# Turned tokens, tables and bias laid out by the host, and a new order of the first loads and splits

## The chip, the cores and the metric

The kernel runs on one core of one Trainium2 chip. The metric is the device time of one execution in microseconds (us), the median of several runs. Engines are named as the profile names them: PE is TensorE (its weight loads are PEld), DVE is VectorE, ACT is ScalarE, POOL is GpSimd, SP is SyncE, which here only issues DMAs.

## The reference

One sequence of 256 tokens, width 1024, fp32 throughout. Two blocks follow each other.

The first block: RMS norm, one projection of 3088 columns, gated linear attention with 4 heads and a block attention with 8 heads, an output projection, RMS norm, and a retrieval layer: 8 heads each take the top 16 of 128 x 128 product keys, gather the 16 rows of `peer_u` and `peer_v` for each token (4 KB a row), and add `gate * gelu(u.x) * v`.

```
x = first_block(x, ...)
  xn = rmsnorm(x, norm1_w); proj = xn @ w_in
  o_gla, o_moba from proj;  x += concat(o_gla, o_moba) * mix_scale @ w_out
  q = rmsnorm(x, norm2_w) @ w_query; s = q . subkeys; top-16 of 128, twice; top-16 of 256
  x += sum_k gate_k * gelu(u_k . xn) * v_k
x = second_block(x, ...)
  twice: mixer, then conv-GLU feed-forward (1024 -> 2 x 2816 -> 1024), then
         x += sigmoid(rmsnorm(x) @ ple_gate) * (p @ ple_proj)
```

The mixer of the second block's first layer is stick-breaking attention beside HGRN2; that of its second layer is a sliding-window attention whose logits get a bias from a table of 32 distance buckets for each of 16 heads. The feed-forward's convolution has three taps and a bias for each column.

## The kernel before, in words

All matrix products are done in two halves of a number: an operand is split into `hi` (rounded, type fp32r) and `lo = x - hi`, and `product` sums three matmuls, hi*hi, hi*lo and lo*hi (lines L2093 to L2095). Weights arrive as pieces of 1 MB (128 partitions x 2048 numbers) in four slots. A piece goes through a fixed chain: SP loads it (`load`, L468), ACT rounds it to `hi` (`split`, L436), DVE (`split_lo`, L443) or POOL (`split`, L591) makes `lo`, PE uses it. A slot is loaded again when the old piece's `hi` and `lo` are made, and rounded again when PE has used the old piece. Each engine works through one list written out by hand, in order; `PLAN` gives each PE job a number, its PSUM bank is that number modulo 8, and `pe_done` and `evac_done` count the jobs.

The tokens' root of the mean square is not needed before the products: it is multiplied in when a product is taken from PSUM (`root_col`, L1338).

The start, in the order of PE's list: the norm weights, loaded as 72 rows by six DMAs of ACT's queue, are turned (L2157); the 256 x 1024 tokens are turned by 16 transposes (`norm_T`, L2058); eight spins (L2052, matmuls with no use but to keep PE at work); the first projection tile of both halves of the tokens (`dense_tile("win", 0, t)`), the 16-column gate projection ("gr"), the turning of the convolution's taps (L2171), the one-hot product that spreads the bias table (L2174), then win tile 1 of the first tokens, alpha (L2179), win tile 1 of the second tokens, and so on. ACT meanwhile takes the squares and roots of the tokens (`norm_root`, L801 to L811), rounds the turned tokens (L832), and the pieces.

Six projection chunks of two pieces each are made: pieces 0 and 1 are split by DVE, 2 and 3 by POOL, 4 and 5 by DVE, 6 and 7 by POOL, 8 to 11 by DVE. DVE's list: `early_tables` (takes gr, taps and bias row, and waits for the constants and for eight small tables that SP broadcasts to all partitions, `gain_loaded`), the splits of 4 and 5, `gla_gate`, `gla_log_gate` and the query norms and rotation `moba_qk` (L1395 to L1418), the splits of 8 and 9, the same for the keys, the splits of 10 and 11.

The bias row of 16 heads is written out 128 times to a scratch tensor in device memory (L499) and read back skewed at the second layer (L570). The sub-keys are loaded in their own layout and turned by PE in four jobs ("subk", "subk_rest"), copied by DVE (L1574) and ACT (L946). The side input `p` is turned by PE at the end of each feed-forward (job "pT", `ple`), copied from PSUM to `PHI` and subtracted into `PLO` by DVE (L1940, L1941). There POOL makes `lo` of the side projection's weights (`ple_proj_lo`, L591).

## Time and profile before

| | |
|---|---|
| median of 3 runs | 1551.3 us (1549.95 to 1555.15) |
| the profiled execution | 1546.3 us |
| its span, first to last instruction | 1544.5 us |
| PE, DVE, ACT, POOL busy | 90, 67, 46, 40% of the span |
| DMA moved | 415 MB, 269 GB/s on average |

The profile is of one execution. A row of the timeline gives the start, the length and the instruction with how often it follows itself; a row of the chain of waits gives one step of the work that ended last.

### The profile page before, as it was taken

The numbers are of one execution on the slowest core, as the hardware profiler recorded it, in microseconds if no ns is written. First come the engines' busy times: TensorE is split into PE (matmuls) and PEld (weight loads), VectorE is DVE, ScalarE is ACT, GpSimd is POOL, SyncE is SP. The second block draws the span as 40 slices with busy tenths as digits, with TensorE's granted clock in tenths as the row PEclk, the third lists the DMA queues.
The fourth block names the chain that finished last, engine by engine and source line by source line (L and its number), as shares of the span: only waits on it lengthen the run. The fifth ranks groups of instructions, "written<-read, shape, count | busy, mean of one in ns | idle before, by whom it ended". The sixth has DMA issues, their size and how long they took to land.

```text
span 1544.5 us, 18260 instructions
## 1 busy us (share of the span) xinstructions
PE 1388.1 (90%) x5985; PEld 969.8 (63%) x5985; DVE 1028.5 (67%) x1916; ACT 711.6 (46%) x1381; POOL 620.2 (40%) x581
## 2 busy tenths in 40 slices
PE   7989998787788867778789999999999999999998
PEld 6877973333333323333335879788888778888887
DVE  4895786666666766666664547669863586498733
ACT  5534643233322333333334372477645755776534
POOL 2330777433433333333362521045443512364414
PEclk9999999889999999998899999999999999999999
DMA  9287599999999999999999601557665443476650
GB/s 312 89 138 231 211 339 411 421 422 421 422 422 422 421 422 422 422 421 422 421 413 348 198 32 50 164 165 217 190 218 175 162 139 104 125 207 195 215 192 28
DMA packets 187076, 415.00 MB, mean 269 GB/s; under 512 B 9882, under 2 KB 113922, under 8 KB 160386
## 3 DMA queue, kind: packets, MB, share of 16 engines
q0 software_dynamic: 43776, 268.45, 42.4%
q1 hardware_dynamic: 143090, 145.66, 30.8%
q8 instruction: 38, 0.62, 0.2%
q14 instruction: 28, 0.23, 0.0%
q10 hardware_dynamic: 144, 0.04, 0.0%
HBM read 409.93 MB, written 4.19 MB: 268 GB/s over the span
## 4 chain that ended last, share of the span: by engine, by line
PE 51%; DMA 21%; DVE 10%; ACT 6%; POOL 6%; issue 5%; ACTq 0%; POOLq 0%; DVEq 0%; SPq 0%
DMA expert_rows<-in_peer_uv,route_idx 20%; PE ps L2380 10%; PE ps L2549 10%; PE ps L2093 7%; PE ps L2095 7%; PE ps L2094 7%; PE ps L2550 5%; DVE weights_lo L443 2%; POOL expert_rows L674 2%; POOL weights_lo L591 2%; ACT weights_hi L436 2%; PE ps L2058 1%; DMA weights_raw<-in_ab_w_in 1%; POOL ple_proj_lo L591 1%; ACT scratch L981 1%
## 5 line engine op out<-in xcount | busy, mean ns | idle before, releaser
L1677 DVE CUSTOM_DVE_ANT_0 expert_rows<-expert_rows,ps 128x1024 f32<-128x1024 f32 x184 | 224.1, 1220 | 147.0 <-DMA expert_rows<-in_peer_uv,route_idx 131.7
L591 POOL TENSOR_TENSOR weights_lo<-weights_raw,weights_hi 128x512 fp32r<-128x512 f32 x120 | 160.0, 1366 | 370.2 <-ACT weights_hi L436 328.1
L2380 PE MATMUL ps<-expert_rows,scratch 128*128 128x512 f32 x512 | 246.2, 639 | 58.4 <-ACT scratch L981 55.0
L674 POOL DMA_INDIRECT expert_rows<-in_peer_uv,route_idx x156 | 147.3, 944 | 225.9 <-PE ps L2380 189.6
L436 ACT CAST weights_hi<-weights_raw 128x2048 fp32r<-128x2048 f32 x98 | 185.5, 1917 | 106.4 <-PE ps L2095 79.8
L2380 PEld LDWEIGHTS ps<-expert_rows,scratch 128*128 128x128 f32 x512 | 102.1, 204 | 201.6 <-issue 124.6
L2549 PE MATMUL ps<-x_normT,weights_hi 128*128 128x512 f32 x640 | 222.5, 393 | 0.0
L443 DVE TENSOR_TENSOR weights_lo<-weights_raw,weights_hi 128x2048 fp32r<-128x2048 f32 x68 | 160.9, 2373 | 74.2 <-ACT weights_hi L436 73.8
L2093 PE MATMUL ps<-weights_hi,x_normT 128*128 128x512 f32 (+1 forms) x496 | 188.3, 380 | 9.3 <-DVE weights_lo L443 3.7
L967 ACT ACTIVATE proj<-proj 128x4 f32<-128x4 f32 x64 | 13.2, 205 | 397.8 <-DVE proj L1677 397.8
L2095 PE MATMUL ps<-weights_hi,x_normT 128*128 128x512 f32 (+1 forms) x496 | 184.7, 372 | 0.0
L2094 PE MATMUL ps<-weights_lo,x_normT 128*128 128x512 f32 (+1 forms) x496 | 184.6, 372 | 0.0
L2550 PE MATMUL ps<-x_normT,weights_lo 128*128 128x256 f32 x640 | 178.3, 279 | 0.0
L2380 PE MATMUL ps<-expert_rows,proj 128*128 128x512 f32 x288 | 135.7, 627 | 25.7 <-ACT proj L981 25.1
L2549 PEld LDWEIGHTS ps<-x_normT,weights_hi 128*128 128x128 f32 x640 | 119.9, 187 | 27.1
L2380 PEld LDWEIGHTS ps<-expert_rows,proj 128*128 128x128 f32 x288 | 56.6, 200 | 104.1 <-issue 68.8
L2550 PEld LDWEIGHTS ps<-x_normT,weights_lo 128*128 128x128 f32 x640 | 120.6, 188 | 0.0
L2093 PEld LDWEIGHTS ps<-weights_hi,x_normT 128*128 128x128 f32 x496 | 93.4, 188 | 31.0 <-issue 4.2
L2095 PEld LDWEIGHTS ps<-weights_hi,x_normT 128*128 128x128 f32 x496 | 93.4, 188 | 16.6
L2094 PEld LDWEIGHTS ps<-weights_lo,x_normT 128*128 128x128 f32 x496 | 93.5, 189 | 15.5 <-issue 0.2
L2380 PE MATMUL ps<-work_a,proj 128*128 128x512 f32 x112 | 65.5, 739 | 36.3 <-ACT proj L981 36.3
L1905 DVE SCALAR_TENSOR_TENSOR work_a<-ps,conv_cols,work_a 128x254 f32<-128x254 f32 (+1 forms) x176 | 76.4, 475 | 29.3 <-ACT work_a L1120 25.1
(365 smaller groups left out, 2452.5 us busy)
## 6 DMA issues: line engine op xcount, KB each, us to landing
weights_raw<-in_ffn_up SPq DMA_DIRECT2D x88, 512.0 KB, 5.0
weights_raw<-in_ffn_down SPq DMA_DIRECT2D x22, 1024.0 KB, 4.9
weights_raw<-in_ab_w_in SPq DMA_DIRECT2D x14, 1024.0 KB, 6.0
weights_raw<-in_w_in SPq DMA_DIRECT2D x12, 1024.0 KB, 8.0
weights_raw<-in_ple_gate SPq DMA_DIRECT2D x8, 1024.0 KB, 6.2
weights_raw<-in_c_w_in SPq DMA_DIRECT2D x6, 1024.0 KB, 5.9
weights_raw<-in_w_out SPq DMA_DIRECT2D x4, 1024.0 KB, 12.8
weights_raw<-in_peer_w_query SPq DMA_DIRECT2D x4, 1024.0 KB, 12.5
```

The costliest lines, as they stand in the source:

```text
L436: copy(w.hi[:, :], w.raw[:, :]).then_inc(hi_ready[w.h], 1)
L443: eng.tensor_tensor(w.lo[:, :], w.raw[:, :], w.hi[:, :].bitcast(F32), ALU.subtract).then_inc(lo_ready[w.h], 1)
L591: ins = pool.tensor_tensor(w.lo[:, c], w.raw[:, c], w.hi[:, c].bitcast(F32), ALU.subtract)
L674: nc.gpsimd.indirect_dma_start(out=dst, out_offset=None, in_=table, in_offset=bass.IndirectOffsetOnAxis(ap=r_idx[:, q, n:n + 1], axis=0)). ...
L1677: ins = nc.vector.tensor_tensor_reduce(out=rows, in0=rows, in1=tokens, scale=1.0, scalar=0.0, op0=ALU.mult, op1=ALU.add, accum_out=r_dot[: ...
L1905: ins = nc.vector.scalar_tensor_tensor(out=d, in0=PS[:, (j0 + 2 * q + g) % 8, 0:S - n], scalar=CONV[:, l, bass.ds(i * RING + (tap * 2 * FT ...
L2093: pe.matmul(o, x[0], w[0], start=first, stop=False)
L2094: pe.matmul(o, x[0], w[1], start=False, stop=False)
L2095: return pe.matmul(o, x[1], w[0], start=False, stop=last)
L2380: ins = pe.matmul(PS[:, (J[f"peer_{t}"] + m) % 8, :], DIAG[b][:, k, :], rows[:, m * BANK:(m + 1) * BANK], start=False, stop=False, skip_gr ...
L2549: pe.matmul(b.rearrange("p (a t) -> p a t", a=2), hi[:, c, g, :], x_both(c), start=c == 0, stop=False)
L2550: ins = pe.matmul(b[:, 0:S], lo[:, c, g, :], XHI[:, c, :], start=False, stop=c == KC - 1)
```

## The change

The host prepares seven arrays (`laid_out`): the tokens turned (1024 rows of features), the norm weights as 72 columns, the taps and their bias as columns, the sub-keys turned, `p` turned, the whole banded window bias (128 x 16 x 256), and the table of `u` and `v` rows side by side, which was there before. On the chip the turnings by PE, their copies out of PSUM, the scratch tensor and its write are gone.

- Start: SP loads turned tokens in two halves, then win pieces 0 to 3, then the tokens in rows, then gr, alpha and all constants, then pieces 4 and 5, then the taps, the eight broadcast tables, the levels and pieces 6 to 11. ACT's queue has one DMA in place of six.
- ACT rounds the turned tokens (8 instructions of 128 x 256), then pieces 0 and 1 in quarters of 512 columns, then pieces 2 and 3 whole, then squares and roots, then the 16-column weights, then 4 and 5. DVE follows with the quarters of `lo`.
- PE: six matmuls on the turned tokens whose result is overwritten, then the first tile, each step as its quarter becomes ready.
- POOL splits pieces 2, 3 and 7; DVE splits 6, ahead of `gla_log_gate`.
- alpha goes to two banks, one for each half of the tokens.
- `PHI` and `PLO` are made from the loaded `p` in SBUF.
- The sub-keys' load goes ahead of the wait for `mb_O1`, and query piece 5 no longer waits for PE's turning of the sub-keys. The second layer's bias is one plain load.

```diff
-            sp.dma_start(C[:, 0:P], a["c_small"][:, 0:P]).then_inc(sem("ident_loaded"), 16)
-            for t in range(TT):
-                sp.dma_start(X[:, t, :], a["x"][0, t * P:(t + 1) * P, :]).then_inc(sem(f"x_loaded{t}"), 16)
+            for half in range(2):
+                cols = slice(4 * half, 4 * half + 4)
+                sp.dma_start(XCOLS[:, cols, :], a["x_cols"][:, cols, :]).then_inc(sem(f"x_cols_loaded{half}"), 16)
             for p in halves(0):
                 load("win", p)
+            for p in halves(1):
+                load("win", p)
+            for t in range(TT):
+                sp.dma_start(X[:, t, :], a["x"][0, t * P:(t + 1) * P, :]).then_inc(sem("x_loaded"), 16)
             sp.dma_start(W_GR, cols512(w_in, 1536, GRANK)).then_inc(sem("gr_loaded"), 16)
             sp.dma_start(W_ALPHA, a["gla_w_alpha"][0]).then_inc(sem("gr_loaded"), 16)
-            for p in halves(1):
+            sp.dma_start(C[:, :], a["c_small"]).then_inc(sem("const_loaded"), 16)
+            for p in halves(2):
                 load("win", p)
...
-            for p in (*halves(1), *halves(3)):
+            for p in (2, 3, 7):
                 split("win", p)
...
+            act.wait_ge(sem("vec_loaded"), 16)
+            for f in range(KC):
+                if f % 4 == 0:
+                    act.wait_ge(sem(f"x_cols_loaded{f // 4}"), 16)
+                nc.scalar.activation(XHI[:, f, :], XCOLS[:, f, :], ACT.Copy,
+                                     scale=VEC[:, NORM_COL[0] + f:NORM_COL[0] + f + 1]).then_inc(sem("first_hi"), 1)
+            for half in halves(0):
+                w = pieces["win", half]
+                act.wait_ge(raw_loaded[w.r], w.landed)
+                for c in range(4):
+                    cols = slice(c * BANK, (c + 1) * BANK)
+                    act.copy(w.hi[:, cols], w.raw[:, cols]).then_inc(hi_ready[w.h] if c == 3 else sem("first_hi"), 1)
+            for p in halves(1):
+                split("win", p)
             for t in range(TT):
-                norm_root(0, t, (sem(f"x_loaded{t}"), 16), (sem(f"x_loaded{t}"), 16))
...
+                norm_root(0, t, (sem("x_loaded"), 32), (sem("x_loaded"), 32))
...
             def moba_queries():
+                split_lo(v, "win", 6)
                 gla_log_gate()
                 moba_qk(0)
...
-                j = J[f"pT{l}"]
-                src = bank(j).rearrange("p (c t) -> p c t", c=2)
-                step(nc.vector.tensor_copy(PHI[:, :, :], src))
-                freed(nc.vector.tensor_tensor(PLO[:, :, :], src, PHI[:, :, :].bitcast(F32), ALU.subtract), j)
+                v.wait_ge(sem("p_loaded"), 16 + 16 * l)
+                step(nc.vector.tensor_copy(PHI[:, :, :], PIN[:, l]))
+                nc.vector.tensor_tensor(PLO[:, :, :], PIN[:, l], PHI[:, :, :].bitcast(F32), ALU.subtract).then_inc(sem("p_split"), 1)
...
+            b = bank(tile_job("win", 0, 0))
+            pe.wait_ge(sem("x_cols_loaded0"), 16)
+            for _ in range(6):
+                pe.matmul(b[:, 0:S], XCOLS[:, 0, 0:P], XCOLS[:, 0, :], start=True, stop=True)
+            for f in range(KC):
+                w, c = pieces["win", f // 4], f % 4
+                pe.wait_ge(*((lo_ready[w.h], w.count) if c == 3 else (sem("first_lo"), KC + 3 * (f // 4) + c + 1)))
+                hi, lo = part(w.hi, 4), part(w.lo, 4)
+                ins = product(b, xs(f, slice(0, P)), (hi[:, c, :], lo[:, c, :]), f == 0, f == KC - 1)
+            ins.then_inc(pe_done, 1)
+            dense_tile("win", 0, 1)
```

## Rows read from the trace of the kernel before

**Rows 1.** The page: shares of the span in the chain of waits, by engine.
```profile
PE 51%; DMA 21%; DVE 10%; ACT 6%; POOL 6%; issue 5%; ACTq 0%; POOLq 0%; DVEq 0%; SPq 0%
```

**Rows 2.** Stage table: stretch, length, busy us of each engine, PEclk, DMA share, GB/s.
```profile
4.00:11.00 7.00, 2.59 (x13) 2.62 (x14) 0.53 (x3) 5.75 (x19) 0.00 (x0) 1.00 1.05 392
...
20.00:24.00 4.00, 4.00 (x20) 3.30 (x19) 1.89 (x4) 1.35 (x1) 4.00 (x4) 1.00 0.35 72
...
300.00:800.00 500.00, 394.02 (x818) 163.02 (x817) 335.64 (x842) 155.08 (x501) 193.53 (x206) 0.92 1.01 421
```

**Rows 3.** Timeline, the first tokens' work and gr: start us, length us, engine, line.
```profile
5.54 0.63 ACT L801 ACTIVATE x_norm<-x_res 128x512 f32<-128x512 f32 x1 [0.58 <-DMA x_res<-in_x]
...
8.55 3.62 PE L2058 MATMUL ps<-consts,x_res 128*128 128x128 f32 x16
...
8.95 0.29 ACT L811 ACTIVATE stats<-stats 128x1 f32<-128x1 f32 x1
...
17.34 0.41 ACT L855 CAST w_gr_hi<-scratch 128x128 fp32r<-128x128 f32 x1
...
19.18 0.43 SPq L492 DMA_DIRECT2D sink_rows<-in_sinks  x1
...
20.26 0.88 DVE L1378 TENSOR_TENSOR w_gr_lo<-scratch,w_gr_hi 128x128 fp32r<-128x128 f32 x1
```

**Rows 4.** Chain of waits, 0 to 60 us: start us, length us, what.
```profile
26.82 0.12 PE ps L2093
...
29.63 0.30 PE ps L2171 x4
...
30.68 0.43 PE ps L2093
```

**Rows 5.** DMA issues, 0 to 215 us: KB each, us from issue to landing.
```profile
sink_rows<-in_sinks SPq DMA_DIRECT2D x1, 8.0 KB, 6.3
```

**Rows 6.** Timeline of DVE and ACT, 28 to 90 us.
```profile
43.19 0.75 DVE L1338 TENSOR_SCALAR proj<-ps,stats 128x512 f32<-128x512 f32 x1 [3.69 <-PE ps L2095]
...
48.91 1.70 DVE L1404 TENSOR_TENSOR proj<-proj,stats 128x512 f32<-128x512 f32 x1
...
58.84 0.69 DVE L1404 TENSOR_TENSOR proj<-proj,stats 128x512 f32<-128x512 f32 x1
...
62.55 1.41 DVE L1338 TENSOR_SCALAR proj<-ps,stats 128x512 f32<-128x512 f32 x2
63.88 4.48 DVE L443 TENSOR_TENSOR weights_lo<-weights_raw,weights_hi 128x2048 fp32r<-128x2048 f32 x2
...
43.17 3.72 ACT L436 CAST weights_hi<-weights_raw 128x2048 fp32r<-128x2048 f32 x2 [1.07 <-PE ps L2095]
```

**Rows 7.** Timeline of POOL, 18 to 90 us: the splits of pieces 2, 3 and 6, 7.
```profile
19.69 10.08 POOL L591 TENSOR_TENSOR weights_lo<-weights_raw,weights_hi 128x512 fp32r<-128x512 f32 x8 [19.23 <-ACT weights_hi L436]
45.23 12.50 POOL L591 TENSOR_TENSOR weights_lo<-weights_raw,weights_hi 128x512 fp32r<-128x512 f32 x8 [15.46 <-ACT weights_hi L436]
```

**Rows 8.** Timeline of the first side input, DVE and (last row) one POOL instruction.
```profile
1198.24 0.67 DVE L1940 CAST ple_hi<-ps 128x512 fp32r<-128x512 f32 x1
1198.95 0.69 DVE L1941 TENSOR_TENSOR ple_lo<-ps,ple_hi 128x512 fp32r<-128x512 f32 x1
1200.04 3.08 DVE L443 TENSOR_TENSOR weights_lo<-weights_raw,weights_hi 128x2048 fp32r<-128x2048 f32 x1 [0.40 <-ACT weights_hi L436]
...
1200.93 3.34 POOL L591 TENSOR_TENSOR ple_proj_lo<-ple_proj_raw,ple_proj_hi 128x512 fp32r<-128x512 f32 x1
```

**Rows 9.** Chain of waits at the first side input.
```profile
1199.73 7.05 POOL ple_proj_lo L591 x4
```

**Rows 10.** Timeline: PE behind the sub-keys and behind the side input, first gather.
```profile
163.36 0.36 PE L2093 MATMUL ps<-weights_hi,x_normT 128*128 128x256 f32 x1 [0.29 <-DVE x_normT L1325]
...
173.51 1.11 POOL L661 DMA_INDIRECT expert_rows<-in_peer_u,route_idx  x1 [4.38 <-DVE route_idx L1639]
...
1194.65 0.47 PE L2093 MATMUL ps<-weights_hi,x_normT 128*128 128x512 f32 x1 [0.34 <-DVE x_normT L1325]
```

More of the change, by code:

```diff
@@ L1368, in _ @@
             step(nc.vector.memset(SS[:, 95:96], EPS), "eps_ready")
-            freed(nc.vector.tensor_copy(VEC[:, :], bank(J["vecs"])[:, 0:72]), J["vecs"], wait=True)
+            for f in range(KC):
+                v.wait_ge(sem("first_hi"), f + 1)
+                nc.vector.scalar_tensor_tensor(out=XLO[:, f, :], in0=XCOLS[:, f, :],
+                                               scalar=VEC[:, NORM_COL[0] + f:NORM_COL[0] + f + 1],
+                                               in1=XHI[:, f, :].bitcast(F32), op0=ALU.mult,
+                                               op1=ALU.subtract).then_inc(sem("first_lo"), 1)
+            for half in halves(0):
+                w = pieces["win", half]
+                for c in range(4):
+                    cols = slice(c * BANK, (c + 1) * BANK)
+                    v.wait_ge(*((hi_ready[w.h], w.count) if c == 3 else (sem("first_hi"), KC + 3 * half + c + 1)))
+                    nc.vector.tensor_tensor(w.lo[:, cols], w.raw[:, cols], w.hi[:, cols].bitcast(F32),
+                                            ALU.subtract).then_inc(lo_ready[w.h] if c == 3 else sem("first_lo"), 1)
             for t in range(TT):
@@ L1372, in _ @@
             v.wait_ge(sem("norm_rstd"), rstd_no[0])
-            for half in range(2):
-                norm_lo(0, 0, (half,))
-                split_lo(v, "win", half)
-            norm_lo(0, 1)
             v.wait_ge(sem("gr_hi_ready"), 1)
@@ L1878, in vec_ffn @@
                 norm_lo(k, 1)
+                v.wait_ge(sem("conv_loaded"), 16)
                 j0 = J[f"up{l}"]
@@ L2297, in _ @@
             spin(J["wout"], 3)
-            def subkeys(j, m):
-                pe.wait_ge(sem("subkeys_loaded"), 16)
-                transposes(j, [SKN[:, 4 * m + n, :] for n in range(4)])
             def head_tokens(t, j):
@@ L2594, in ple @@
             def ple(l, k):
-                pe.wait_ge(sem("p_loaded"), 16 + 16 * l)
-                transposes(J[f"pT{l}"], [PIN[:, l, t, c * P:(c + 1) * P] for c in range(2) for t in range(TT)])
                 dense_tile(f"gate{l}", 0, 0, normed(k, 0))
```

148 lines of the change are left out of this document (49 added, 99 removed), and 4 rows, old and new, of the table PLAN.

## The prediction

> **What bounds the kernel now.** I read the shares of the chain of waits first. PE carries half of it and DMA a fifth [rows 1], so the span is made of stages with different owners. The table by stage shows that from 300 to 800 us the DMA engines are full, share 1.01 at 421 GB/s [rows 2]: this is the gather of expert rows, which the change does not touch. Its first gather is issued at 173.5 us, when the first indices are there [rows 10]. Whatever the change gains or loses ahead of that point moves the gather as a block, and the rest with it; behind it only the edits at the side inputs count. So there are two questions: how much sooner the indices come, and what happens at 1200 and 1516 us.
>
> Ahead of the gather the chain is PE from 26.8 us on without a pause [rows 4], then from about 62 us DVE: it takes the product of win chunk 2 only at 62.55 us, though PE had it earlier, because it was in the query norms from 43.19 us on [rows 6]. The end of win tile 1 at E = 42.9 us (just ahead of the 43.19 row) is the hinge: I work out how E moves, then how long DVE needs from E to its 62.55.
>
> **The start, to win tile 1.** Before, gr starts at 26.82, ends at 29.63, taps and bias row take to 30.68, and then win tile 1 starts [rows 4]. In the changed kernel the first tiles come sooner, but I find that they don't set the time. gr needs the 16-column weights in two halves, and on ACT these now stand behind the roots of the tokens, and the tokens' rows load behind four pieces. Bytes up to the last token row: 1 MiB turned tokens + 4 MiB pieces + 1 MiB rows = 6.29 MB. At the 392 GB/s of 4 to 11 us [rows 2], with 2.0 us until the first byte, the last arrives at 2.0 + 16.1 = 18.1. Before, 64 KB of constants and half a MiB had to arrive for the first root at 5.54 [rows 3]: 2.0 + 0.59 MB / 392 = 3.5, so up to 2 us between byte and use; I take 1.5: 19.6. The two roots took 5.54 to 9.24, 3.7 us; the hi 0.41, the lo 0.88 [rows 3]: 24.6, PE at 24.7. gr is 2.8 long: 27.5, and nothing is left between it and win tile 1. So tile 1 starts at 27.5 in place of 30.68: **-3.1 us** (bounds -4 and -1.5, from a lag of 0.6 to 3.1 us).
>
> Do the two first tiles end ahead of 24.7? The turned tokens land near 5 us; the norm columns, one DMA, by about 6. Eight roundings of about 0.4, then quarters of half a us as piece 0 and 1 land (2.1 and 3.1 MB: near 9 and 12 us), lo behind them: PE begins near 12, is fed the last quarter near 16, and is through both tiles (48 matmuls of 0.227, the spacing in the chain) near 23. Two us of slack. POOL has piece 2 from about 16.5 on; at 10.08 for two pieces [rows 7] both are ready at 27, in time for the first and second half of tile 1. So all of the chunked start, its early norm table and the six extra matmuls cost and bring nothing here: the roots hide them.
>
> **The small tables, later now.** The eight broadcasts stood ahead of pieces 4 and 5 and now stand behind them. Before, the last was issued at 19.18 and took 6.3 us [rows 3, 5]: 25.5, at a time when DMA was nearly empty, share 0.35 over 20 to 24 [rows 2]; so they are slow by themselves. DVE waits for all eight ahead of its splits of 4 and 5. After: gr, alpha, constants, pieces 4 and 5 are 2.9 MB behind the rows, with taps end of bytes near 26, then 4 to 5 us for the eight. I take G = 30.6. Behind G on DVE: two splits 4.6, one evacuation 0.75, gate 0.87, absolute value 0.69; on ACT two functions and a table load 2.6: G + 9.5. ACT can only round piece 6 behind it, and PE frees its slot at E = 39.8. So G matters from 30.3 on, one for one; **+0.5 us** (bounds 0 and +2).
>
> **Piece 6 from POOL to DVE.** Before, from 43.19 to 62.55, DVE is 19.4 us, of which one and the same instruction of the query norms takes 1.70 us beside POOL's splits and 0.69 when POOL is done [rows 6, 7]. Reading it as waiting for the POOL instruction under way fits: each of the six instructions beside POOL is about one us longer. With 6 on DVE, POOL has 4 instructions in place of 8. But DVE must wait for ACT's hi (1.9 behind the hinge) and work 2.29 (half of the 4.48 row) ahead of everything, until E + 4.4; POOL's four for piece 7 (ready at E + 3.8) then alternate with DVE's next ones (log gate, scaling, square), each of which waits 1.25 until POOL's is through. From E: 4.4, then 6.2, 7.9, 10.3, sums to 11.8, root and reciprocal 12.3, two halves of norm and rotation 3.7 each: 19.7. Before it was 19.6. **0 us**: split and saved waits cancel. Bounds: +0.3, and -2.8 if nothing waits for POOL any more (6.2 us of waits gone, 3.4 us of split and its wait added). I stay at the upper end, since the alternation is what the 1.70 row shows. PE's list behind it (chunks 2 to 4, until about E + 36) stays ahead of DVE, as before.
>
> The Trainium skill (SBUF — State Buffer, "Who interferes with whom") says that DVE and GpSimd take a shared pair of ports as an exclusive lock: an instruction of DVE with two SBUF inputs, or a plain copy in a two-port mode, waits for a GpSimd one that reads SBUF, or the other way round, for its whole length. The rows agree: 1.70 is 0.69 plus most of a POOL instruction. By that rule the term is 0; by a view in which the engines share bandwidth it would be negative.
>
> **The side inputs.** POOL's four instructions on the side projection are on the chain, 7.05 us [rows 9], and again at the second side input, where the row is alike. Without a wait they would take 5.04, as half the 10.08 of rows 7; the rest is one of 3.34 us that sat behind DVE's split of 3.08 [rows 8]. Before, DVE's two instructions ahead of it (0.67 and 0.69) read PSUM, and POOL passed beside them. After, both read SBUF alone. The copy waits for POOL's instruction, 0.2, runs about 0.35; POOL's last on the gate piece starts that much late, ends near 1200.0; the subtraction waits for it, runs to 1200.7; POOL's first of four starts there in place of 1199.7; DVE's split waits for that, runs to 1204.2; POOL's other three end at 1208.0, where they ended at 1206.8. **+1.2 at each, +2.4 in all**; bounds 0 (no wait at all) and +1.3 each. As DVE and POOL may fall into a better order, I take 1.0 each: **+2.0 us**. PE had 0.3 us or less to spare there. By the skill's rule the copy from SBUF takes the pair as well; if it did not, the subtraction alone would cost 0.7 to 0.9 each.
>
> **Edits at nothing.** The sub-keys' turning: PE waited 0.29 us for DVE's norm behind it, ahead of the query products [rows 10], so that wait hides it; 0. The turning of `p`: PE waited 0.34 for DVE behind it [rows 10]; 0. The scratch write and the bias load have no waiter in the chain; the plain load is of the same size, 2 MB. DVE's and ACT's copies of the sub-keys stood ahead of waits for PE. Query piece 5's earlier load: its hi waits for PE, not for the load. alpha in two banks: 0. The sub-keys' load stands ahead of query piece 4 on SP, 1 MB or 2.6 us of DMA, in a stretch with no wait for pieces.
>
> **Sum.** -3.1 + 0.5 + 0 + 2.0 = -0.6 us on the execution of 1546.3; on the median of 1551.3, which is 5.0 above it and has the same stages, that is 1550.7. Extremes: -4.0 - 2.8 = -6.8, and -1.5 + 2.0 + 0.3 + 2.6 = +3.4. A measurement of this kernel tells about 0.3%, 4.7 us, from no change.
>
> **Rivals.**
> - **POOL and DVE do not get in each other's way as I say.** Then piece 6 brings -2.8 and the side inputs cost 0: -3.1 + 0.5 - 2.8 = -5.4, 1545.9. For it: POOL's instructions halve beside the norms, and 1.0 us each was paid there six times. Against it: the 3.34 row, and that the split has to be worked off somewhere. If the lag of the rows is short too, 1545.0.
> - **The tables come late and DVE becomes the bound from there (slower).** Place: DVE's wait for the eight tables ahead of the splits of 4 and 5. From G = 30.3 each us counts; break-even with the start's gain, side inputs included, is at G = 31.4 (-3.1 + 2.0 = -1.1 to be eaten), and at G = 36 the sum is -1.1 + 5.7 = +4.6, 1555.9. For it: they needed 6.3 us with an empty DMA, and are now queued behind 2 MB of pieces. Against it: SP issues them well ahead of their bytes, so that most of this runs beside the pieces' bytes.
> - **PE's clock stays low.** Before, the 16 transposes take 3.62 us, 0.226 each [rows 3], the spacing of the lower level (1.2 GHz), before the products run at the upper one; the granted clock column shows 1.00 all the same. After, PE has a pause ahead of the products, waits between quarters, and waits 2 us ahead of gr. If the two tiles and gr all ran at the lower level, 48 matmuls of 0.454 and 24 of 0.234 from 12 us on, win tile 1 would start at 39.4, +8.7, in all +10.7 with the side inputs: 1562. It decides once the level rises later than about 2 us, the slack, behind the first product. The skill (TensorE: Matmul & The Clock Gate, "HAM oscillation — how this bites in real kernels") says that pauses of PE bring back the half rate; here the pauses are short, so I give it little.
> - **The start gains more:** the roots of the tokens don't hold gr. Then tile 1 starts near 26 and the sum is -2.
>
> **Chances.** My forecast and the small variants around it (1547 to 1553, its own range) 0.60; the first rival 0.22; late tables 0.12; low clock 0.04; something not listed 0.02. Faster by over 0.3%: most of the first rival and a tail of the forecast, 0.27. Slower by over 0.3%: half of the late tables' cases, the clock, a tail of the forecast: 0.13. Within 0.3%: 0.60. The range takes in the first rival's time and the upper sum: 1544.5 to 1555.0.
>
> **What would show it.** Win tile 1 starting near 27.5 us, with PE waiting some 2 us ahead of gr for DVE's lo of the 16-column weights; if PE doesn't wait there, the first step is wrong. DVE's wait for the tables ending between 29 and 32. DVE taking chunk 2 about 19.7 us behind the end of win tile 1: 2 or 3 us sooner speaks for the first rival. The first gather at about 171 in place of 173.5. POOL's four side-projection instructions ending 1 us later than their place in the stage before, twice. If the first gather comes at 168 or sooner, the prediction is wrong in the start; if the stretch from first gather to end is shorter than before, it is wrong in the side inputs or in an edit that I priced at nothing.

## The result: slower by some 5 us, and the profile after

The kernel after takes 1555.8 us (median of 10 runs) against 1551.4 us: ratio 1.0033 with a 95% interval of 1.0022 to 1.0044. A second comparison gave 1.0039 [1.0026, 1.0053]. That is 3.4 to 8.2 us slower; the forecast was 1550.7 us, no change, with a range of 1544.5 to 1555.0. Two executions far outside the rest, 3216 us (x_first, below) and 1739 us (before), were marked slow and are in no ratio.

The two profiled executions are further apart than the medians, 1556.7 us with a span of 1554.9 against 1546.3 and 1544.5. Before reading anything from that, it has to be known what one kernel does from one execution to the next; the first two experiments are on that.

The page of after, shares of the chain of waits [rows 1]:

```profile
PE 47%; DMA 21%; DVE 10%; POOL 7%; ACT 7%; issue 6%; SPq 1%; another core or an unknown queue 0%; POOLq 0%; DVEq 0%; ACTq 0%
```

PE has lost 4 points, and SP's issuing, at 0 before, has 1. Part of that is the start, where the chain no longer runs over PE. The chain of waits of after from 0 to 70 us, at the places where [rows 4] had PE alone (start, length, what):

```profile
8.87 7.25 SPq L490
...
23.23 13.00 DMA sink_rows<-in_sinks
...
38.52 2.28 DVE weights_lo L453
...
42.27 0.70 DVE work_a L1442
...
45.58 1.81 ACT weights_hi L446
47.51 2.29 DVE weights_lo L453
...
61.75 0.70 DVE proj L1410
```

Up to 23 us the chain is SP's own issues, one of which (the alpha weights, behind the 1024 short rows of the 16-column weights) held it for 7.25 us; then it is the last of the eight small tables, 13.0 us from issue to landing where [rows 5] had 6.3; then it is DVE's list, with ACT's two functions and one split between. PE, which was the chain here before, is not in it at all.

The timeline of after: ScalarE, PE and then DVE, which answer to [rows 3, 4, 6] (start, length, instruction, idle time before it and what ended that):

```profile
19.76 0.63 ACT L801 ACTIVATE x_norm<-x_res 128x512 f32<-128x512 f32 x1 [1.00 <-DMA x_res<-in_x]
...
25.14 0.29 PE L2093 MATMUL ps<-x_normT,w_gr_hi 128*16 128x256 f32 x1 [3.79 <-DVE w_gr_lo L1387]
29.50 0.40 PE L2093 MATMUL ps<-weights_hi,x_normT 128*128 128x512 f32 x1
...
23.76 1.32 DVE L1387 TENSOR_TENSOR w_gr_lo<-scratch,w_gr_hi 128x128 fp32r<-128x128 f32 x1
...
36.30 4.49 DVE L453 TENSOR_TENSOR weights_lo<-weights_raw,weights_hi 128x2048 fp32r<-128x2048 f32 x2 [6.19 <-DMA sink_rows<-in_sinks]
...
47.51 2.29 DVE L453 TENSOR_TENSOR weights_lo<-weights_raw,weights_hi 128x2048 fp32r<-128x2048 f32 x1 [3.75 <-ACT weights_hi L446]
49.72 1.78 DVE L1446 SCALAR_TENSOR_TENSOR work_a<-work_a 128x512 f32<-128x512 f32 x1
...
57.31 0.69 DVE L1409 TENSOR_TENSOR proj<-proj,stats 128x512 f32<-128x512 f32 x1
...
64.73 1.41 DVE L1339 TENSOR_SCALAR proj<-ps,stats 128x512 f32<-128x512 f32 x2
```

Win tile 1 starts at 29.50 instead of 30.68, so the start without the turnings did bring PE 1.2 us. But DVE stands idle until 36.30 for the tables, and takes chunk 2 at 64.73 us instead of 62.55 [rows 6]. The first gather follows at 175.53 instead of 173.51 [rows 10].

The stage table of after, to set beside [rows 2] (stretch, length, busy us of each engine, PEclk, DMA share, GB/s):

```profile
24.00:28.00 4.00, 2.86 (x15) 2.01 (x16) 2.40 (x3) 2.81 (x2) 2.23 (x2) 0.68 0.90 311
28.00:32.00 4.00, 4.00 (x22) 3.14 (x21) 0.41 (x1) 2.27 (x2) 0.00 (x0) 0.89 0.16 45
32.00:36.00 4.00, 4.00 (x18) 2.91 (x16) 0.00 (x0) 0.00 (x0) 0.00 (x0) 1.00 0.47 166
...
300.00:800.00 500.00, 389.28 (x813) 160.90 (x812) 336.74 (x849) 153.00 (x493) 192.88 (x204) 0.93 1.01 421
```

While DVE waits for the tables, the DMA engines are busy for 16 and then 47% of the time and move 45 and then 166 GB/s: the stream stands, though the engines are mostly idle. The first and the last of the eight, in the list of DMA issues of after (KB, us from issue to landing):

```profile
gain_rows<-in_gla_out_norm_w SPq DMA_DIRECT2D x1, 64.0 KB, 8.3
...
sink_rows<-in_sinks SPq DMA_DIRECT2D x1, 8.0 KB, 13.0
```

They were issued at 19.30 and 23.23 us, so they landed at 27.6 and 36.2: the eight took 8.6 us. The gather from 300 to 800 us is the same as before.

At the first side input, DVE of after and then its chain of waits, beside [rows 8, 9]:

```profile
1207.11 0.52 DVE L1942 CAST ple_hi<-work_b 128x512 fp32r<-128x512 f32 x1
1207.66 1.67 DVE L1943 TENSOR_TENSOR ple_lo<-work_b,ple_hi 128x512 fp32r<-128x512 f32 x1
...
1208.79 7.48 POOL ple_proj_lo L591 x4
```

The subtraction takes 1.67 us beside POOL instead of 0.69. From SP's load of the side input to its first load of `c_w_out` is 66.87 us (1174.10 to 1240.97) instead of 66.30 (1165.22 to 1231.52); from the second such load to the end of the span 63.7 (1491.21 to 1554.9) instead of 62.8 (1481.67 to 1544.5). The first stretch repeats within 0.1 us and the second within 0.4 us in every profile with the same code there, so the side inputs cost 0.6 + 0.9 = 1.5 us.

### The profile page after: what moved, and what is told of

The parts are those of the page before. It is cut to its first block, busy times and chain, and to the rows that moved or that the text cites. A ratio compares the mean times of both kernels' runs of the same rounds, so it can differ in the third digit from the quotient of the medians.

```text
span 1554.9 us, 18114 instructions
## 1 busy us (share of the span) xinstructions
PE 1386.0 (89%) x5934; PEld 967.1 (62%) x5934; DVE 1027.0 (66%) x1916; ACT 710.2 (46%) x1381; POOL 617.8 (40%) x577
## 4 chain that ended last, share of the span: by engine, by line
PE 47%; DMA 21%; DVE 10%; POOL 7%; ACT 7%; issue 6%; SPq 1%; another core or an unknown queue 0%; POOLq 0%; DVEq 0%; ACTq 0%
DMA expert_rows<-in_peer_uv,route_idx 11%; PE ps L2538 9%; PE ps L2369 9%; DMA scratch<-in_peer_uv,route_idx 8%; PE ps L2093 6%; PE ps L2095 6%; PE ps L2094 6%; PE ps L2539 5%; DVE weights_lo L453 2%; POOL weights_lo L591 2%; ACT weights_hi L446 2%; POOL expert_rows L642 1%; POOL expert_rows L674 1%; PE ps L2060 1%; POOL expert_rows L661 1%
## 5 line engine op out<-in xcount | busy, mean ns | idle before, releaser
L591 POOL TENSOR_TENSOR weights_lo<-weights_raw,weights_hi 128x512 fp32r<-128x512 f32 x116 | 154.5, 1366 | 373.1 <-ACT weights_hi L446 331.0
L2369 PE MATMUL ps<-expert_rows,scratch 128*128 128x512 f32 x512 | 240.3, 625 | 57.9 <-ACT scratch L981 57.9
L446 ACT CAST weights_hi<-weights_raw 128x2048 fp32r<-128x2048 f32 x96 | 181.7, 1915 | 93.4 <-PE ps L2095 74.6
L2369 PE MATMUL ps<-expert_rows,proj 128*128 128x512 f32 x288 | 138.5, 635 | 27.9 <-ACT proj L981 22.3
L2538 PEld LDWEIGHTS ps<-x_normT,weights_hi 128*128 128x128 f32 x640 | 119.9, 187 | 27.1
L1908 DVE SCALAR_TENSOR_TENSOR work_a<-ps,conv_cols,work_a 128x254 f32<-128x254 f32 (+1 forms) x176 | 76.5, 475 | 29.6 <-ACT work_a L1121 25.5
```

Source lines behind the costliest of these rows:

```text
L446: copy(w.hi[:, :], w.raw[:, :]).then_inc(hi_ready[w.h], 1)
L591: ins = pool.tensor_tensor(w.lo[:, c], w.raw[:, c], w.hi[:, c].bitcast(F32), ALU.subtract)
L1908: ins = nc.vector.scalar_tensor_tensor(out=d, in0=PS[:, (j0 + 2 * q + g) % 8, 0:S - n], scalar=CONV[:, l, bass.ds(i * RING + (tap * 2 * FT ...
L2369: ins = pe.matmul(PS[:, (J[f"peer_{t}"] + m) % 8, :], DIAG[b][:, k, :], rows[:, m * BANK:(m + 1) * BANK], start=False, stop=False, skip_gr ...
L2538: pe.matmul(b.rearrange("p (a t) -> p a t", a=2), hi[:, c, g, :], x_both(c), start=c == 0, stop=False)
```

## Experiments

Each ratio is to executions of the kernel before made beside it, 8 to 12 executions of the variant, of spins 5; before_again was only profiled. The medians of before in these comparisons lie between 1545.5 and 1552.6 us, so ratios are compared here and not times. "Chunk 2" is the time at which DVE takes the product of win chunk 2, where the prediction's working of the start ends; "tables" is when DVE's wait for the tables ends.

| kernel | tables us | chunk 2 us | ratio to before | interval |
|---|---|---|---|---|
| before, first profile | no wait | 62.55 | 1 | |
| before_again | no wait | 62.44 | | |
| after, first profile | 36.30 | 64.73 | 1.0033 | 1.0022 to 1.0044 |
| after_again | 35.67 | 64.14 | 1.0039 | 1.0026 to 1.0053 |
| gains_pool | no wait | 67.45 | 1.0044 | 1.0031 to 1.0057 |
| p6_pool | 36.67 | 64.62 | 1.0019 | 1.0006 to 1.0031 |
| gains_mid | no wait | 64.45 | 1.0021 | 1.0007 to 1.0034 |
| x_first | 36.78 | 65.22 | 1.0030 | 1.0016 to 1.0044 |
| ple_early | as after | 64.75 | 1.0029 | 1.0017 to 1.0041 |
| combined | no wait | 63.32 | 1.0005 | 0.9991 to 1.0020 |
| gains_host | no wait | 61.38 | 1.0016 | 1.0005 to 1.0027 |
| gr_host | 35.46 | 63.89 | 1.0035 | 1.0022 to 1.0048 |
| before_gains_host | no wait | 62.52 | 1.0002 | 0.9992 to 1.0011 |
| best | no wait | 60.09 | 0.9997 | 0.9984 to 1.0010 |
| before_late | 32.67 | 62.07 | 1.0001 | 0.9991 to 1.0011 |
| spins | 37.05 | 65.44 | 1.0050 | 1.0037 to 1.0064 |
| best_spins | 28.38 | 58.65 | 0.9988 | 0.9976 to 1.0000 |
| before_late_extra | 34.64 | 62.58 | 1.0003 | 0.9989 to 1.0017 |

### What varies by itself: before_again, after_again

> The kernel before, unchanged, for a second profile. In the first one GpSimd had no pause of 3.3 us among the gathers and its own time was 1546.3 us, 5 us below its median; the kernel after had two such pauses and 1556.7 us. Theory A (the pauses come and go from run to run): here too GpSimd has one or more such pauses (their number differs from zero in at least one of two further profiles), and the stretch from the first gather to the last differs from the first profile's 644.0 us by about 3.3 us for each. Theory B (the change causes them): none here, stretch 644.0 within 0.5 us.

> The kernel after, unchanged, for a second profile and a closer ratio. Theory A (pauses vary from run to run): another number of pauses than two is likely, and the stretch from first to last gather follows it at 3.3 us each; start (first gather at 175.5) and side inputs repeat within 0.3 us. Theory B (the change causes them): two pauses again at the same places (242.96 and 265.92 us). The ratio stays at 1.0022 to 1.0044: start +2.0 and side inputs +1.5 us are read from the first traces, so +3.5 us is accounted for, and a ratio of 1.0023 would be all of that.

Theory A holds in that the pauses come and go. POOL's timeline in before_again has two, which the first profile of before lacked:

```profile
259.99 0.94 POOL L642 DMA_INDIRECT expert_rows<-in_peer_v,route_idx  x1 [5.33 <-remote]
...
808.64 0.94 POOL L674 DMA_INDIRECT expert_rows<-in_peer_u,route_idx  x1 [3.38 <-remote]
```

after_again has two as well, at other places than after. From first to last gather before_again took 650.5 us, after_again 650.4, against 644.0 and 650.8 in the first profiles. So the 7 us by which the first pair of traces differ there are no effect of the change. Over the 18 profiles of this study the stretch lies between 643.5 and 646.0 us in the five without a pause, and between 648.1 and 654.3 in the thirteen with one or two, for variants of either kernel. It does not follow the number of pauses at 3.3 us each, as I had expected.

The first gather did not repeat either: 173.41 in after_again instead of 175.53, 171.85 in before_again instead of 173.51. From chunk 2 to the first gather it is 109.2 to 109.4 us in ten profiles and 110.8 to 111.0 in eight, of either kernel; what decides between the two is open. So a single first gather tells nothing under 2 us, but what chunk 2 gains or loses does arrive at the gather in full. What can be read from single traces is the start up to chunk 2, which repeats within 0.6 us, and the stretches around the side inputs.

### The tables: gains_pool, gains_mid, gains_host, before_gains_host

gains_pool moves the loop of eight broadcasts to GpSimd's queue, at its very start:

```
-                sp.dma_start(dst, src[0].partition_broadcast(P)).then_inc(sem("gain_loaded"), 16)
+                pool.dma_start(dst, src[0].partition_broadcast(P)).then_inc(sem("gain_loaded"), 16)
```

> The kernel after with the eight broadcast tables issued on GpSimd's queue at the start instead of on SyncE's behind pieces 4 and 5. Theory (the late tables are what made the start slower): DVE's wait for them, which ended at 36.2 us, goes; the scores of the gate then wait for alpha (35.0) alone, so only 1 to 1.5 us of the head's path comes back at the gate but DVE's splits of pieces 4 and 5 (4.49 us), which stood behind the tables, move ahead of alpha's end to 30 or so, and DVE's exponentials chain starts 4 to 5 us sooner: first gather at 171 to 172.5 instead of 175.5, time 3 to 4.5 us less than after. Rival (the rest of the chain, ACT's pieces 6 and 7 and GpSimd's half-speed splits, holds it): the first gather moves by less than 1.5 us. Rival of cost: the eight issues at the start slow the first token and weight loads: first product later than 10.1 us.

The theory failed here and the rival of cost came true; the first gather came at 176.83, later than in after. The stage table of gains_pool, in the columns of the one above:

```profile
8.00:12.00 4.00, 1.72 (x6) 1.08 (x4) 0.92 (x3) 0.33 (x1) 0.00 (x0) 1.00 0.91 93
12.00:16.00 4.00, 0.00 (x0) 0.00 (x0) 0.00 (x0) 0.00 (x0) 0.00 (x0) 0.54 0.94 153
```

The DMA engines are over 90% busy and move only 93 and 153 GB/s, and the first weight pieces crawl. From this queue the eight took 9.9 us from the first landing to the last, the longest of all. (On SyncE's queue the engines are not kept busy by them, see the 16% above; the stream stands all the same.) All compute engines stand still from 12 to 16 us; gr comes 7.8 us later than in after, chunk 2 only 3 us later, because the tables no longer stand in the way there.

gains_mid puts the loop ahead of the constants and pieces 4 and 5, on SyncE.

> The kernel after with the eight broadcast tables issued on SyncE ahead of the constants and pieces 4 and 5 (at some 16.2 us instead of 19.3), behind the token and weight loads of the first two tiles. In the trace of after the last of them lands 12.3 us behind... 17 us after the first's issue; on GpSimd's queue at the start they took 15.7 us, so their transport costs some 10 us wherever it stands. Theory (late tables): DVE's wait ends at 28 to 33 us instead of 36.2, the first gather comes 1.5 to 3.5 us sooner than in after (175.5 and 173.4 in its two profiles), the time is 1.5 to 3.5 us less. Rival (the small rows hold back pieces 4 and 5, which now land later than 36 us): DVE waits for the high parts of pieces 4 and 5 instead, no gain, within 1 us of after.

The rival holds for the start. ScalarE of gains_mid:

```profile
33.52 1.91 ACT L446 CAST weights_hi<-weights_raw 128x2048 fp32r<-128x2048 f32 x1 [9.43 <-DMA weights_raw<-in_w_in]
```

Now piece 4 is late instead, and its `lo` and piece 5's are made as late as behind the tables; chunk 2 is taken at 64.45, the same as after. The ratio of 1.0021 is 2.3 us below after's, of which chunk 2 shows nothing. Neither place in this queue makes the cost go away. What might is to make the transfer fast:

```
-                sp.dma_start(dst, src[0].partition_broadcast(P)).then_inc(sem("gain_loaded"), 16)
+            for dst, cols in ((GAIN[:, :], slice(0, 512)), (ALB[:, :], slice(512, 768)), (SINK[:, :], slice(768, 784))):
+                sp.dma_start(dst, a["gain_tab"][:, cols]).then_inc(sem("gain_loaded"), 16)
```

> The kernel after with the eight broadcast tables laid out by the host as one array of 128 equal rows, 392 KB, loaded at the same place in SyncE's order in three DMAs of whole rows (2 KB, 1 KB and 64 B per partition). Theory B (the tables' slow transport, some 9 us at 45 to 166 GB/s while everything behind them waits in the same queue, is what the start lost): DVE's wait for them ends at 28 to 30 us instead of 36.2, pieces 4 and 5 are split by 35.5, the gate's values leave DVE 5 to 6 us sooner, chunk 2 is taken at 58 to 61 us instead of 64.1 to 64.7, and the time is 3 to 6 us less than after, at or below the kernel before. Rival (TensorE's order from 29.5 us on holds it: idle ahead of gr, low granted clock): chunk 2 taken at 63 us or later, under 1.5 us gained.

DVE of gains_host:

```profile
29.79 4.47 DVE L453 TENSOR_TENSOR weights_lo<-weights_raw,weights_hi 128x2048 fp32r<-128x2048 f32 x2
...
42.11 0.75 DVE L1337 TENSOR_SCALAR proj<-ps,stats 128x512 f32<-128x512 f32 x1 [4.53 <-PE ps L2093]
...
61.38 1.41 DVE L1337 TENSOR_SCALAR proj<-ps,stats 128x512 f32<-128x512 f32 x2
```

The wait is gone, DVE now waits for PE (4.53 us), and chunk 2 comes 3.1 us sooner than in the two profiles of after (mean 64.4), at 61.38 just short of the 58 to 61 expected. The ratio falls from 1.0036 (the mean of after's two) to 1.0016, 3 us, the least that was expected, and not to the kernel before or below it; the intervals overlap slightly, so it is the trace, more than the ratio, that shows the gain. 392 KB in three transfers of 128 rows each, equal in content but each with its own place in memory, pass in the stream, which stays at 382 to 386 GB/s from 26 to 32 us; in eight broadcasts of one row each they took 8 to 9 us of it.

> The kernel before, with the tables laid out by the host as above. Theory B: in the kernel before the tables took DMA time too (72 GB/s from 20 to 24 us) ahead of pieces 4 and 5, whose splits started at 32.3 and 35.0 us, but TensorE reached its second win tile only at 30.7 us and its end at 42.9 us, so little is gained: 0 to 2 us less. Rival: the data stream bounds this kernel's start as much, 3 to 5 us less, and then the change would have lost nothing by the tables.

In the kernel before the same edit brings nothing: ratio 1.0002, chunk 2 at 62.52. So the tables' cost became a cost through the change.

### What made them late: before_late, before_late_extra, gr_host

before_late gives the kernel before the new order alone, tables behind pieces 4 and 5. before_late_extra also loads the token rows a second time:

```
+            for t in range(TT):
+                sp.dma_start(A[:, t * D:(t + 1) * D], a["x"][0, t * P:(t + 1) * P, :]).then_inc(sem("gain_loaded"), 16)
+            for p in halves(2):
+                load("win", p)
             for dst, src in ((LB_GAIN, ...
```

> The kernel before, with its eight broadcast tables issued behind pieces 4 and 5 as in the kernel after. Theory (the order alone makes them late): DVE, which reads none of them before its wait at 30.8 us, is held until 34 to 36 us, pieces 4 and 5 are split from then on instead of from 32.3, chunk 2 is taken 1 to 3 us later than 62.5, 1 to 3 us slower. Rival (the additional 1 MB of turned tokens, 2.7 us at 380 GB/s, and SyncE's later issues made them late in the kernel after): here the tables land by 32.5 us, chunk 2 is taken within 0.7 us of 62.5, time within 1 us of before.

> The kernel before with its tables behind pieces 4 and 5 (as in the run before this one: wait ended at 32.7 us, chunk 2 taken at 62.1 us, ratio 1.0001) and the token rows loaded a second time, into a place that nothing reads, ahead of pieces 4 and 5: 1 MB more in the queue, as the turned tokens are in the kernel after. Theory (data queue): 1 MB at 380 GB/s is 2.8 us, so DVE's wait ends at 35.3 to 36 us, its gate 2.7 us later, chunk 2 is taken at 63.8 to 65 us, 1.5 to 2.8 us slower than before: ratio 1.001 to 1.002. Rival (slack of 3 us between the gate and DVE's next wait at 42.7 us takes it): chunk 2 within 0.7 us of 62.1, no difference in time, and what the start of the kernel after lost lies in its piece 6 or elsewhere.

DVE of before_late, and then of before_late_extra:

```profile
32.67 4.49 DVE L443 TENSOR_TENSOR weights_lo<-weights_raw,weights_hi 128x2048 fp32r<-128x2048 f32 x2 [1.81 <-DMA sink_rows<-in_sinks]
```

```profile
34.64 4.49 DVE L443 TENSOR_TENSOR weights_lo<-weights_raw,weights_hi 128x2048 fp32r<-128x2048 f32 x2 [3.64 <-DMA sink_rows<-in_sinks]
```

The order alone costs nothing: the rival holds. The megabyte puts the tables 2.0 us later, somewhat less than the 2.8 expected, and that too costs next to nothing, which I had not expected: chunk 2 at 62.58. The reason is in the table at the head of the experiments. Wherever the tables bind, chunk 2 comes a fixed time behind them: 28.4 us with piece 6 on DVE (after, after_again, gr_host, x_first, spins: 28.39 to 28.47), 27.9 us with it on POOL (p6_pool and before_late_extra: 27.95 and 27.94). So in the kernel before the tables have room until 62.5 - 27.9 = 34.6, just where before_late_extra put them, and every us beyond is lost. The kernel after has them at 35.7 to 36.3, and its own PE would have allowed 61.4 - 28.4 = 33.0.

What brought them there is not the bytes ahead of them alone. Issue times and the lists of DMA issues give the landings of the first and the last of the eight:

| kernel | first lands, us | last lands, us | between |
|---|---|---|---|
| before, before_again | 21.3, 21.5 | 25.5, 26.0 | 4.2, 4.5 |
| before_late | 26.2 | 32.4 | 6.2 |
| before_late_extra | 28.6 | 34.5 | 5.9 |
| after, after_again | 27.6, 27.6 | 36.2, 35.6 | 8.6, 8.0 |
| the seven other variants of after with the eight on SyncE | 20.2 to 27.7 | 28.3 to 37.0 | 8.0 to 9.3 |

In before_late_extra the first table lands later than in after, and the last one sooner. At the 5.9 to 6.2 us of the two variants of before, after's tables would have landed at 33.5 to 33.8, close to the edge (an estimate: 27.6 plus these). Order and bytes used up the room, and the 2 to 3 us by which the same eight transfers pass more slowly in the kernel after went over the edge. What in the change makes them slower is open: with the same order, and with one more megabyte too, the kernel before does not get there.

gr_host lays out the 16-column weights, so that SP is not held:

> The kernel after with the gate weights' 64 KB laid out by the host too (512 B per partition instead of 1024 rows of 64 B). Theory: the issue behind them, which held SyncE for 7.25 us, falls under 1 us and constants, pieces 4 and 5 and the tables are issued 6 us sooner, but the data queue ahead of them is as full as before, so the tables land at 34 to 36 us instead of 36.2: gr's product starts as before at 24.6 to 25.2 us (the roots are what it waits for) and the time is within 1.5 us of after. Rival (the blocked issue is the cause of the late tables): tables land at 30 us, 3 to 4 us less time.

SP's issue of alpha fell from 7.25 to 1.39 us (under 1 was expected); the tables' wait ended at 35.46, and the ratio stayed, 1.0035. As the theory has it, what stands in the queue decides, not SP.

### PE ahead of gr: x_first, spins

x_first loads the token rows ahead of pieces 2 and 3 and puts the roots ahead of piece 3's split. spins adds between the first tiles and gr:

```
+            for _ in range(7):
+                pe.matmul(b[:, 0:S], XCOLS[:, 0, 0:P], XCOLS[:, 0, :], start=True, stop=True)
```

> The kernel after with the token rows loaded ahead of pieces 2 and 3 on SyncE, and ScalarE's two roots ahead of its split of piece 3. Theory (TensorE's idle 3.8 us ahead of gr and the lower granted clock behind it cost the start): gr's product starts at 21.3 to 22.5 us instead of 25.1, the granted clock stays high from 24 to 30 us, the second win tile starts at 25 to 26.5 instead of 29.5. As long as the tables land at 36.2 us DVE's chain behind them does not move, so the time alone changes by 0 to -1 us. Rival (the start is all on TensorE): first gather 3 to 4 us sooner and the time 3 to 4 us less.

> The kernel after with seven products of no use (turned tokens by themselves, 128x256) between its first two tiles and gr, so that TensorE does not idle from 21.3 to 25.1 us. Theory (the idle time brings the lower clock, the tables hide it): the granted clock from 24 to 30 us is 1.0 instead of 0.5 to 0.87, gr's 24 products take 2.9 us instead of 4.4, the second win tile starts at 27.7 to 28.2 instead of 29.5, but DVE's wait still ends at 36 us and chunk 2 is taken at 64 to 64.8: time within 1 us of after. Rival (the start is on TensorE after all): chunk 2 taken 1 to 2 us sooner, 1 to 2 us less.

x_first missed what it was to test. DVE of x_first:

```profile
24.54 1.25 DVE L1387 TENSOR_TENSOR w_gr_lo<-scratch,w_gr_hi 128x128 fp32r<-128x128 f32 x1 [1.89 <-ACT w_gr_hi L860]
```

The roots were done 1.0 us sooner, but now piece 2 landed later and the 16-column weights, split behind piece 3, took the roots' place. The wait ahead of gr has three things that end it within a us or two of each other. The stage tables of after (from 24 us, above: PEclk 0.68, 0.89) and of spins:

```profile
24.00:26.00 2.00, 1.41 (x10) 0.86 (x9) 2.00 (x3) 1.53 (x1) 2.00 (x2) 1.00 1.05 387
26.00:28.00 2.00, 2.00 (x20) 1.66 (x19) 0.46 (x1) 1.20 (x2) 0.29 (x1) 1.00 0.73 232
```

With PE kept busy, the granted clock stays at 1.00, gr's 24 products take 2.8 us (25.20 to 27.97) instead of 4.4 (25.14 to 29.50) and win tile 1 starts at 27.97, 1.5 us sooner. As expected the tables then hide it. The time was not "within 1 us of after" but 1.0050, 2 us above it, from 5 executions; its profile has the tables at 37.05, 0.8 to 1.4 us later than in the two of after, and why is open.

### Piece 6, side inputs: p6_pool, ple_early

```
-            for p in (2, 3, 7):
+            for p in (2, 3, 6, 7):
...
-                split_lo(v, "win", 6)
```

> The kernel after with piece 6 split on GpSimd again (pieces 2, 3, 6, 7) and none on DVE. Forecast of the prediction's step on it: no difference, because GpSimd's piece 6 (some 6.5 us after ACT's high part) puts piece 7 later by as much as DVE is relieved by 2.3 us: first gather within 0.5 us of 175.5, time within 1.5 us of after. Rival (DVE's 2.3 us stood on the path, as chunk 2 was taken 2.2 us later): 1.5 to 2.8 us faster. Rival (piece 7's end on GpSimd is what the fourth chunk waits for): slower by 1 to 4 us.

Chunk 2 came 27.95 instead of 28.45 us behind the tables: piece 6 on POOL is 0.5 us better at the start, no more. The ratio of 1.0019 is 2.6 us below after's, with intervals that overlap; the profile shows no stage in which such a gain would lie, so I take it as 0.5 us and leave the rest open. That, like the 2.3 us of gains_mid, is nearly as much as the ratio gave for gains_host: a ratio by itself does not tell such differences apart.

> The kernel after with DVE's two operations on the side input (PHI and PLO, 0.52 and 1.67 us) ahead of the residual sums, in DVE's idle time, in both layers. Theory (they stand on the path and are doubled by GpSimd): the stretch from the last gather to the next load landmark shortens by 1 us in each layer, time 1.5 to 2 us less than after. Rival (the stage ends by GpSimd's split of ple_proj): within 0.5 us of after.

ple_early moves the three lines on `PHI` and `PLO` to the head of the function, ahead of the residual sums. DVE of ple_early:

```profile
1176.50 0.42 DVE L1935 CAST ple_hi<-work_b 128x512 fp32r<-128x512 f32 x1
1176.95 0.69 DVE L1936 TENSOR_TENSOR ple_lo<-work_b,ple_hi 128x512 fp32r<-128x512 f32 x1
```

With POOL idle the same two take 0.42 and 0.69. The two stretches are 66.25 and 63.1 us: the first loss is gone, the second down to 0.3. The ratio, 1.0029, is 1 us below after's, less than the 1.5 to 2 expected and within its interval.

### Versions that put it together: combined, best, best_spins

combined is gains_mid + x_first + p6_pool + ple_early; best is gains_host + gr_host + p6_pool + ple_early; best_spins adds the seven products.

> The kernel after with all of it: tables ahead of pieces 4 and 5, token rows ahead of pieces 2 and 3 and the roots ahead of piece 3's split, piece 6 split on GpSimd, side input's operations early. Theory (late tables, the gap ahead of gr and the side inputs are what the change lost, and they hide each other at the start): 5 to 9 us less than after, 1548 to 1553 us, at or below the kernel before. Rival (one of them alone decides): no more than 3 us less than after.

> The kernel after with the tables and the gate weights laid out by the host, piece 6 split on GpSimd, and the side input's two operations ahead of the residual sums. Theory: the gains add where they lie in different stages: start 4 to 6 us, side inputs 1 to 1.5 us, 5 to 8 us less than after, 1 to 3 us less than before. Rival (noise of the gather stage and one shared bound at the start): no faster than before.

> The best kernel so far (tables and gate weights laid out by the host, piece 6 on GpSimd, side input's operations early; ratio 0.9997 to before, chunk 2 taken at 60.1 us) with the same seven products. Theory: with the tables gone TensorE is what DVE waits for (0.8 us at 33.2, 4.5 us at 36.2), so the higher clock now counts: second win tile at 26.5 to 27.2 instead of 28.1, chunk 2 taken at 58.3 to 59.3, 1 to 2 us less than that kernel, 1.5 to 3 us less than before. Rival (DVE's order from 42 us on holds chunk 2): chunk 2 at 60, no gain.

combined came level with before, 4.8 us less than after, just short of the expectation. best took chunk 2 2.4 us sooner than before and measured 0.9997, 6 us less than after as expected, but level with before and not 1 to 3 us below it. PE waits 2.55 us ahead of gr in it and the granted clock is 0.63 from 24 to 28 us; best_spins removes that and has chunk 2 at 58.65, 1.4 us sooner, as forecast. DVE of best_spins:

```profile
28.38 4.49 DVE L453 TENSOR_TENSOR weights_lo<-weights_raw,weights_hi 128x2048 fp32r<-128x2048 f32 x2 [0.93 <-DMA sink_rows<-in_gain_tab]
...
39.30 0.75 DVE L1337 TENSOR_SCALAR proj<-ps,stats 128x512 f32<-128x512 f32 x1 [4.26 <-PE ps L2092]
...
58.65 1.41 DVE L1337 TENSOR_SCALAR proj<-ps,stats 128x512 f32<-128x512 f32 x2
```

Its ratio of 0.9988 [0.9976, 1.0000] is 1.9 us less than before and 7 less than after. Against before the interval reaches 1.0000, so it is the one version that may be faster than before; chunk 2 came 3.9 us sooner than there.

## Why the prediction was wrong, point by point

**The step that failed is "The small tables, later now": "then 4 to 5 us for the eight. I take G = 30.6".** The end of the bytes ahead of them was right within 1 to 2 us (piece 5, the last large one, lands at 27.1). The eight then took until 36.3, 9 us instead of 4 to 5. For the kernel before 4 to 5 was right (4.2 and 4.5 us from the first landing to the last), and behind the pieces it was 6; the mistake was to carry one profile's figure over to another queue as if it were fixed. In my argument against the late tables I also had most of it run beside the pieces' bytes; share 0.35 at 72 GB/s [rows 2] already showed that it does not, and while the eight pass in after, the stream stands. Why they take 8 to 9 us in the kernel after is open. With G = 36.3 in the working, the sum would have been -3.1 + 6.0 + 2.0 = +4.9, 1556.2 us, next to the rival "the tables come late" (G = 36, 1555.9 us); measured was 1555.8. I gave it 12 in 100. The agreement is in part luck, as the next points show. (My own G of 30.6 against a limit of 30.3 gave +0.3, not the +0.5 in the sum.)

**From which G it counts.** I had 30.3; for the kernel after it is 33.0 (gains_host's chunk 2 at 61.38, less 28.4), because PE's tile ended later than I had it. So the tables cost 3.1 us at the start, not the 5.7 of the rival.

**The start, -3.1.** It came as -1.2: win tile 1 started at 29.5, not 27.5. gr began at 25.1, near the 24.7 forecast. PE did wait ahead of gr as I said, for the roots, but 3.8 us and not 2, since the first tiles ended at 21.3 and not 23. gr itself took 4.4 us instead of 2.8 because the clock was at its lower level (1.2 GHz) for part of it. The clock was a rival of mine, but only as a disaster of 10.7 us: I had no small case in the sum. spins and best_spins price it at 1.4 to 1.5 us.

The Trainium skill (TensorE: Matmul & The Clock Gate, "HAM oscillation — how this bites in real kernels") says that pauses of PE bring back the half rate. Here most traces agree: PEclk 0.68 from 24 to 28 us with a pause of 3.8 us ahead of gr, 0.63 with one of 2.55 us (best), 1.00 without one. One does not. The first instruction of gr in best, and then in gains_mid:

```profile
23.94 0.29 PE L2090 MATMUL ps<-x_normT,w_gr_hi 128*16 128x256 f32 x1 [2.55 <-DVE w_gr_lo L1385]
```

```profile
24.55 0.29 PE L2093 MATMUL ps<-x_normT,w_gr_hi 128*16 128x256 f32 x1 [2.60 <-DVE w_gr_lo L1387]
```

In gains_mid the granted clock stays at 1.00 from 22 to 32 us, so the length of the pause alone did not decide it. My "here the pauses are short, so I give it little" was the wrong reading all the same.

**Start together.** Forecast for chunk 2: 62.55 - 3.1 + 0.5 = 59.95. Measured 64.7 and 64.1, mean 64.4. From before: 62.5 - 1.1 (what PE brought, by gains_host) + 3.1 (tables) = 64.5.

**Piece 6, 0.** Right where PE's tile is what DVE waits for; where the tables are, piece 6 on DVE cost 0.5 (p6_pool). From the end of win tile 1 to chunk 2 I had 19.7 against 19.6; gains_host (DVE) has 61.38 - 42.11 = 19.3, best (POOL) 60.09 - 40.75 = 19.3, before 19.4. The alternation is there: 1.78 for the instruction behind the split, 0.69 for the norm's once POOL is done.

**The side inputs, +2.0.** Right in kind, 1.5 in size; ple_early gives most of it back. The rule of the Trainium skill that stood beside this step (SBUF — State Buffer, "Who interferes with whom") holds in these rows too: 1.67 us beside POOL, 0.69 without.

**Edits at nothing.** None shows in the traces: from chunk 2 to the first gather, where the sub-keys and the query pieces lie, both kernels take the same 109.3 or 110.9 us.

**What is open.** Start and side inputs make +1.9 + 1.5 = 3.4 us, the lower end of what was measured (3.4 to 8.2). Over the kernel after and its eleven variants, the ratio lies on average about 1.3 us above what chunk 2 and the side inputs account for, while the three variants of before lie at 0.3 to 0.6. Something of a us or so in this family isn't located; the gather's own variation of 11 us from profile to profile covers it. Open too is why the eight tables pass more slowly in this family.

## What to carry to other kernels

Price a transfer by how long the stream stands while it passes, not by its bytes or by its time from issue to landing, and give that price a wide range: the same eight broadcasts took 4.2 to 9.9 us here. Laid out by the host, the same tables were nearly free. When several small things are put in front of a load that someone waits for, find the time up to which that load has room and add them up against it, rather than judge each alone. And compare two profiles of the same kernel before explaining a difference between profiles of two.

## What the runs showed of the hardware that I had not expected

- Eight broadcasts, 392 KB in all, held up the stream on SyncE's queue for 8.0 to 9.3 us in the kernel after and its variants, and for 4.2 to 6.2 in the kernel before and its variants, with the DMA engines mostly idle (16% busy at 45 GB/s from 28 to 32 us of after). Issued on GpSimd's queue at the start they took 9.9 us, with the engines 91 to 94% busy at 93 to 153 GB/s. 128 laid-out rows of the same content passed without a mark. Row length alone (64 B to 1 KB) is not shown to be the cause: the laid-out version has a 64-byte one too, but joins six into 2 KB. The Trainium skill (DMA: Bandwidth & Descriptors, "Specifications") asks for at least 512 B for the full rate; five of the eight are below, and no run here separates that from the repeated source.
- POOL's issuing of gathers pauses zero to two times in an execution, for 1.5 to 5.3 us each, in variants of either kernel, and nothing in the traces says why. Profiles without a pause had a gather stretch 2 to 11 us shorter than those with one or two.
- SP's issue of a small load stood 7.25 us behind a load of 1024 rows of 64 B, and 1.39 us when that was laid out as 128 rows of 512 B.
